# Query panels of the first block as three products, and the order of the loads around them, in a hybrid attention and expert kernel

## What is computed

```python
h = rms_norm(x, g_mix)
proj = h @ w_in
u_ssm, q, k, v, qi, ki, wi, qm, gates = jnp.split(proj, offs, axis=-1)
...
km, vm = jnp.split(rms_norm(mem, g_mem) @ w_mem_kv, 2, axis=-1)
...
merged = g_s * (y_ssm @ w_up_ssm) + g_d * (y_dsa @ w_up_dsa) + g_m * (y_mem @ w_up_mem)
x = x + merged @ w_out
...
```

## Time and profile before

| | us |
|---|---|
| median of 3 runs | 1965.04 |
| lowest, highest | 1964.48, 1965.8 |
| the profiled execution | 1964.33 |
| its span, first to last instruction | 1962.5 |

### The profile page before, as it was taken

How to read it: one execution, slowest core, us unless ns; L and a number is a source line. 1 busy time by engine, 2 the same in 40 slices (tenths; PEclk the granted TensorE clock), 3 DMA queues, 4 the chain that set the end, 5 groups by cost and what they waited for, 6 DMA issues and landing times.

```text
span 1962.5 us, 30069 instructions
## 1 busy us (share of the span) xinstructions
PE 1849.4 (94%) x12400; PEld 1424.3 (73%) x12400; DVE 1157.0 (59%) x1494; ACT 840.2 (43%) x1029; POOL 79.8 (4%) x72
## 2 busy tenths in 40 slices
PE   8998999877787779999999999999999999999998
PEld 5467886444454445888888788888888888788887
DVE  7997577433333335555687476555554688386454
ACT  5346632222121225343556645344443558555331
POOL 2642000000000000000000000000000000000000
PEclk9999999998898989999999999999999999999999
DMA  9479679999999997564454355464555445264552
GB/s 340 124 165 256 202 284 379 420 420 420 421 420 421 420 419 285 192 214 150 157 189 172 108 192 197 167 204 153 202 182 192 162 152 193 89 218 168 192 175 104
DMA packets 166921, 467.05 MB, mean 238 GB/s; under 512 B 9808, under 2 KB 21328, under 8 KB 142080
## 3 DMA queue, kind: packets, MB, share of 16 engines
q1 hardware_dynamic: 152144, 435.07, 59.8%
q0 software_dynamic: 13024, 26.81, 6.2%
q10 hardware_dynamic: 1616, 3.24, 0.5%
HBM read 557.36 MB, written 1.05 MB: 285 GB/s over the span
## 4 chain that ended last, share of the span: by engine, by line
PE 76%; DMA 19%; ACT 3%; DVE 1%; issue 1%; SPq 0%; DVEq 0%; ACTq 0%
PE ps L1042 25%; PE ps L1052 19%; PE ps L1051 19%; DMA ring<-in_w_down 12%; DMA ring<-in_w_up 5%; PE ps L1212 3%; PE ps L1557 2%; PE ps L1576 2%; PE ps L1180 1%; PE ps L1181 1%; DMA raw<-in_w_in 1%; PE ps L1281 1%; DMA raw_r<-in_w_in 1%; PE ps L1526 1%; PE ps L1337 1%
## 5 line engine op out<-in xcount | busy, mean ns | idle before, releaser
L2442 DVE TENSOR_TENSOR w_lo<-raw,w_hi 128x2048 fp32r<-128x2048 f32 x152 | 333.8, 2208 | 126.7 <-ACT w_hi L1879 118.9
L1879 ACT ACTIVATE w_hi<-raw 128x2048 fp32r<-128x2048 f32 x152 | 279.7, 1849 | 227.4 <-PE ps L1042 193.0
L1052 PE MATMUL ps<-w_hi,a_lo 128*128 128x512 f32 (+1 forms) x992 | 374.7, 378 | 0.0
L1042 PE MATMUL ps<-w_hi,a_hi 128*128 128x512 f32 (+1 forms) x960 | 367.1, 382 | 0.2 <-DVEq L2482 0.2
L1051 PE MATMUL ps<-w_lo,a_hi 128*128 128x512 f32 (+1 forms) x920 | 346.4, 377 | 0.0
L1557 PE MATMUL ps<-ring,W 128*32 128x256 f32 x3008 | 192.0, 404 | 55.9 <-DMA ring<-in_w_up 54.7
L1052 PEld LDWEIGHTS ps<-w_hi,a_lo 128*128 128x128 f32 x992 | 186.6, 188 | 34.9
L1042 PEld LDWEIGHTS ps<-w_hi,a_hi 128*128 128x128 f32 x960 | 180.7, 188 | 34.6 <-issue 2.7
L1557 PEld LDWEIGHTS ps<-ring,W 128*32 128x32 f32 x3008 | 95.5, 115 | 138.4 <-DMA ring<-in_w_up 64.7
L1051 PEld LDWEIGHTS ps<-w_lo,a_hi 128*128 128x128 f32 x920 | 173.3, 188 | 30.7 <-issue 0.2
L2442 DVE TENSOR_TENSOR y_lo<-raw,y_hi 128x2048 fp32r<-128x2048 f32 x50 | 114.6, 2292 | 48.3 <-ACT y_hi L1879 45.7
(11 more groups left out here) (479 smaller groups left out, 2858.2 us busy)
## 6 DMA issues: line engine op xcount, KB each, us to landing
ring<-in_w_gate SPq DMA_DIRECT2D x94, 1024.0 KB, 22.5
ring<-in_w_up SPq DMA_DIRECT2D x94, 1024.0 KB, 26.1
ring<-in_w_down SPq DMA_DIRECT2D x94, 1024.0 KB, 22.1
raw<-in_w_in SPq DMA_DIRECT2D x50, 1024.0 KB, 5.1
raw<-in_ffn_w_up SPq DMA_DIRECT2D x44, 1024.0 KB, 5.2
raw<-in_ffn_w_gate SPq DMA_DIRECT2D x42, 1024.0 KB, 5.1
raw<-in_ffn_w_down SPq DMA_DIRECT2D x40, 1024.0 KB, 6.0
raw<-in_w_out SPq DMA_DIRECT2D x10, 1024.0 KB, 5.0
```

Of the source, the lines that this page charges most:

```text
L1042: return released(pe.matmul(dst, a, b, skip_group_check=True, **kw))
L1052: return pe.matmul(dst, a_l, b_h, start=False, stop=final, skip_group_check=True)
L1879: act.activation(E.hi_view(name, ahead), E.raw_view(name, ahead), ACT.Copy).then_inc(hi_split, 1)
L2442: tt(E.lo_view(name, ahead), E.raw_view(name, ahead), E.hi_view(name, ahead).bitcast(F32), ALU.subtract)\
```

## The change

The q and qm units join `CAST_UNITS` ahead of the gates: `scan_piece` multiplies them by `split_products` and waits for the split rows of x (`gate_rows_rest`) and for the unit's accumulating load; SP no longer loads them. The slots of the cast loads are now a table, `CAST_SLOT`, and a load into a slot waits for the unit that last had it. The negations of ACT and the transfers of POOL are placed anew: POOL has one accumulating load ahead of each of tiles 5, 8, 9, 10, 14 and 15 and a cast load ahead of each of tiles 11, 12 and 14. The small loads except the constants and the scan parameters go from ACT's queue to SP's, behind u and km. Late in ACT's order the copies of the turned probabilities come ahead of the copies of gate 3.

```diff
@@ -59,8 +59,9 @@
 PRE_SPLIT = [("up", br, c) for br in ("ssm", "dsa", "mem") for c in range(2)] + [(("wo", c), kh) for c in range(2) for kh in range(2)]
-CAST_UNITS = [(("gate", c), kh) for c in range(6) for kh in range(2)]
+CAST_UNITS = ([(n, kh) for n in ("q", "qm") for kh in range(2)] + [(("gate", c), kh) for c in range(6) for kh in range(2)])
 CAST_SLOTS = 5
+CAST_SLOT = [0, 1, 2, 3, 4, 0, 1, 2, 3, 4, 0, 1, 2, 3, 0, 1]
 IN2 = dict(qa=(0, 512), kva=(512, 256), qb=(768, 512), kb=(1280, 512), vb=(1792, 1024),
@@ -122,6 +123,11 @@
         self.n = start + per * trips
+
+
+def cast_before(j):
+    same = [i for i in range(j) if CAST_SLOT[i] == CAST_SLOT[j]]
+    return len(same), same[-1] if same else None

@@ -819,7 +825,7 @@

-                slot = CAST_UNITS.index(name) % CAST_SLOTS
+                slot = CAST_SLOT[CAST_UNITS.index(name)]
                 hi = [*(w_hi[:, i] for i in range(RAW)), w_lo[:, RAW - 1], a_hi[:, :, :].rearrange("p k s -> p (k s)")][slot]
@@ -957,9 +963,23 @@

+            def small_loads(name):
+
+                if name == ("u", 0):
+                    sp.dma_start(head_rows, A["head_rows"].partition_broadcast(P)).then_inc(rows_loaded, 16)
+                if name == ("u", 1):
+                    sp.dma_start(cc.rearrange("p a t c -> p (a t c)"), A["ssm_c"]).then_inc(c_loaded, 16)
+                    sp.dma_start(bn.rearrange("p a t c -> p (a t c)"), A["ssm_b"]).then_inc(b_loaded, 16)
+                    sp.dma_start(xn[:, :, :], A["mem"].rearrange("a (t p) d -> p (a t) d", p=P)).then_inc(mem_loaded, 16)
+                if name == ("km", 0):
+                    with nc.allow_non_contiguous_dma(reason="positions as a column"):
+                        sp.dma_start(posi[:, :], A["positions"].rearrange("a (t p) -> p (a t)", p=P)).then_inc(pos_loaded, 16)
+                    sp.dma_start(pos_row_i, A["positions"][0].partition_broadcast(P)).then_inc(pos_loaded, 16)
+
             for name in stretch1:
...
                     pre_load(name)
+                small_loads(name)
                 if units.at[name][0] + 1 == gates_used + PRE_RAW:
@@ -1131,9 +1151,22 @@
                     bank((n, t))
+                w, b, dst = unit_shape[name][1], E.pre_view(name), ps[:, bank_of[(n, t)], :]
+                if name in CAST_UNITS:
+                    if t == 0:
+                        pe.wait_ge(gate_rows_rest, 16)
+                        pe.wait_ge(rest_loaded[E.pre_slot(name)], E.pre_loads(name))
+                    hi_, lo_ = E.cast_halves(name)
+                    for k in range(4):
+                        at = (slice(None), 4 * kh + k, slice(t * P, t * P + P))
+                        m = split_products(dst[:, 0:w], g_hi[at], g_lo[at], hi_[:, k, :], lo_[:, k, :], kh == k == 0, kh == 1 and k == 3)
+                    if t == 1:
+                        unit_done()
+                    if kh == 1:
+                        fill(m, (n, t))
+                    return
                 if t == 0:
                     raw_unit(name)
-                w, b, dst = unit_shape[name][1], E.pre_view(name), ps[:, bank_of[(n, t)], :]
                 if n == "km":
@@ -1861,13 +1894,6 @@
             act.dma_start(par[:, 0:3], A["ssm_params"].rearrange("p (a t) -> p a t", a=3)).then_inc(par_loaded, 16)
-            act.dma_start(head_rows, A["head_rows"].partition_broadcast(P)).then_inc(rows_loaded, 16)
-            with nc.allow_non_contiguous_dma(reason="positions as a column"):
-                act.dma_start(posi[:, :], A["positions"].rearrange("a (t p) -> p (a t)", p=P)).then_inc(pos_loaded, 16)
-            act.dma_start(pos_row_i, A["positions"][0].partition_broadcast(P)).then_inc(pos_loaded, 16)
-            act.dma_start(bn.rearrange("p a t c -> p (a t c)"), A["ssm_b"]).then_inc(b_loaded, 16)
-            act.dma_start(xn[:, :, :], A["mem"].rearrange("a (t p) d -> p (a t) d", p=P)).then_inc(mem_loaded, 16)
-            act.dma_start(cc.rearrange("p a t c -> p (a t c)"), A["ssm_c"]).then_inc(c_loaded, 16)

@@ -1881,7 +1907,7 @@
                 n0 = PRE_SPLIT.index(name)
-                earlier = PRE_SPLIT[n0 - RAW] if n0 >= RAW else CAST_UNITS[(7, 10, 11)[n0]]
+                earlier = PRE_SPLIT[n0 - RAW] if n0 >= RAW else CAST_UNITS[(12, 14, 15)[n0]]
                 act.wait_ge(unit_used, E.unit_value(earlier) + 1)
@@ -1891,7 +1917,7 @@
                 j = CAST_UNITS.index(name)
-                act.wait_ge(cast_loaded[j % CAST_SLOTS], j // CAST_SLOTS * 16 + 16)
+                act.wait_ge(cast_loaded[CAST_SLOT[j]], cast_before(j)[0] * 16 + 16)
                 act.wait_ge(unit_used, n0 + 1 - PRE_RAW)
@@ -1988,6 +2014,8 @@
                              scale=r_of["mem" if n in ("km", "vm") else "x"][:, t:t + 1])
+                if i == 0:
+                    minus(("q", 0))
                 if i in (1, 2):
@@ -1996,10 +2024,13 @@
                     act.activation(g_lo[:, :, :], g_hi.bitcast(F32), ACT.Copy, scale=-1.0).then_inc(gate_rows_negated, 1)
+                    minus(("q", 1))
+                    minus(("qm", 0))
                 if i == 2:
+                    minus(("qm", 1))
                     minus((("gate", 0), 0))
+                if i == 3:
                     minus((("gate", 0), 1))
-                if i == 3:
                     minus((("gate", 1), 0))
@@ -2081,8 +2112,8 @@
             minus((("gate", 5), 0))
+            probs_out("dsa", 0, 4, probsT)
             gate(3)
-            probs_out("dsa", 0, 4, probsT)
             minus((("gate", 5), 1))
@@ -3623,9 +3654,9 @@

-                name, slot = CAST_UNITS[j], j % CAST_SLOTS
-                if j >= CAST_SLOTS:
-                    pool.wait_ge(unit_used, units.at[CAST_UNITS[j - CAST_SLOTS]][0] + 1)
+                name, slot = CAST_UNITS[j], CAST_SLOT[j]
+                if cast_before(j)[0]:
+                    pool.wait_ge(unit_used, units.at[CAST_UNITS[cast_before(j)[1]]][0] + 1)
                 pool.dma_start(E.cast_halves(name)[0], unit_source(name, {})).then_inc(cast_loaded[slot], 16)
@@ -3643,8 +3674,25 @@
                         .then_inc(gate_rows_rest, 16)
-                if T in (9, 11, 13):
-                    add_raw((T - 9) // 2)
+                if T == 5:
+                    add_raw(0)
+                if T == 8:
+                    add_raw(1)
+                if T == 9:
+                    add_raw(2)
+                if T == 10:
+                    add_raw(3)
+                if T == 11:
+                    pool.wait_ge(gate_rows_rest, 16)
+                    pool.wait_ge(unit_used, E.unit_value(("kvi", 1)) + 1)
+                    cast_load(4)
+                if T == 12:
+                    cast_load(5)
+                if T == 14:
+                    add_raw(4)
+                    cast_load(6)
+                if T == 15:
+                    add_raw(5)
                 pool.wait_ge(done["scanned"], nth("scanned", T))
@@ -3655,15 +3703,13 @@

-            pool.wait_ge(gate_rows_rest, 16)
-            pool.wait_ge(unit_used, E.unit_value(("qm", 1)) + 1)
-            cast_load(CAST_SLOTS - 1)
-            add_raw(3)
-            cast_load(CAST_SLOTS)
-            for j in range(4, len(CAST_UNITS)):
+            add_raw(6)
+            cast_load(7)
+            cast_load(8)
+            for j in range(7, len(CAST_UNITS)):
+                add_raw(j)
                 if j + 2 < len(CAST_UNITS):
                     cast_load(j + 2)
-                add_raw(j)

```

## The result

The changed kernel takes 1991.84 us at the median (1989.18 to 1992.35), the kernel before 1965.42 us (1964.48 to 1966.51), four runs of each on the same chip: a ratio of 1.0135, 95% interval 1.0123 to 1.0147. The change costs 26.4 us, where the prediction said 17; the time lies 0.8 us above its range. Direction and mechanism held, the size did not. The lowest of the four runs, 1989.18, is inside the range: that the median is just outside may be chance, that it is 10 us above the forecast is not. The profiled execution's span is 1990.5 us, 28.0 longer than before.

What follows compares the result with a forecast made beforehand. TensorE and VectorE were taken as full before 120 us, with TensorE's shift carried to the end. Waits, with savings inside, made 15.7 us, clock 1.7: 17.4 later, forecast 1982 us; term bounds 1974 to 1991, stated range 1968 to 1991.

Steps and rivals of the forecast that it cites:

- What bounds it: Before 120 us TensorE and VectorE are full; a TensorE shift before 300 us reaches the end neither grown nor shrunk.
- Start: At u's product: fewer loads share the DMA, so u's second half starts sooner; gain 1.5 us (0.5 to 1.85).
- The products: At q and qm: a unit takes 5.67 us instead of 7.1; four units save 5.6 us of TensorE.
- Wait 1: Before q, at about 80 us: TensorE waits 3.5 us (2 to 5) for the split rows' transfer.
- Waits 2 and 3: Late casts delay negations ahead of q's and qm's copies: TensorE waits 7.8 us before qm; VectorE's head work starts 15.8 late.
- The clock: In the first stretch: one loss at reduced clock after the new waits, 1.7 us (0 to 5).
- Gate 0 during wait 3: While VectorE waits for qm's copy, TensorE runs gate 0 to about 142 us, then waits for the head rows.
- Behind that: After the head rows: gate 5's negation ahead of the probabilities' copies makes second scores 16.7 us late, then 15.7 late.
- (1): Faster: casts are down before ScalarE needs them, as the scan does not hold POOL; 1958 to 1961 us, chance 0.06.
- (2): No change: wait before qm halved, next small, gate 0's accumulating loads offset the saving; 1961 to 1969 us, chance 0.06.
- (3): Smaller loss: cast 6 lands before qm is full; gate 0's accumulating loads still hold TensorE; 1969 to 1974 us, chance 0.09.
- (4): Larger loss: POOL's queue after the scan sets each later gate, negations hold ScalarE; above 1991 us, chance 0.06.

Runs made afterwards that it cites:

- e12: Changed kernel with only q as products, qm raw, copies before negations, rows' transfer at tile 5, q's first accumulating load at tile 3, late orders restored: 1961.26 us.
- e4: Changed kernel with gate 0's sums in banks 2 and 3 instead of 4 and 5, the banks qm fills: 1990.65 us.
- e5_rows_early: Changed kernel with the transfer of the split rows issued at scan tile 5 instead of 7: 1987.18 us.
- e2_loads_only: Kernel before with only the small loads moved from ACT's queue to SP's: 1965.24 us.
- e1_copies_first: Changed kernel with ScalarE's copies of q ahead of gate 0's negations and copies of qm ahead of gate 1 half 0's negation: 1980.87 us.
- e6_warm: Changed kernel with 44 unused products of the identity into a free bank where TensorE waits for the copy of qm: 1990.49 us.
- e3: Changed kernel with the negation of gate 5 half 0 moved behind the copies of the turned probabilities: 1987.06 us.
- e10: Kernel before with the probabilities' copies ahead of gate 3's copies and, after the scan, each POOL accumulating load ahead of the next cast: 1968.90 us.
- e7: Changed kernel with copies ahead of gate 0 and 1 negations, rows' transfer at tile 5, gate 5 half 0's negation behind the probabilities' copies: 1975.05 us.
- e8: e7 with POOL's cast and accumulating loads also issued earlier, such as cast 4 a tile sooner: 1969.93 us.
- e9_swap_only: Kernel before with only the copies of the turned probabilities moved ahead of the copies of gate 3: 1965.20 us.

## Why the prediction was wrong

Landmarks, in us of the profiled execution:

| | forecast | after |
|---|---|---|
| start gained | 1.5 | 0.36 |
| first q product | 84.0 | 85.22 |
| cast 4 issued, landed | 99.9, 106.6 | 103.38, 110.34 |
| first qm product | 109.2 | 112.91 |
| cast 6 issued, landed | 121.3, 131.3 | 127.19, 137.62 |
| head work begins | 134.6 | 141.09 |
| head rows turned | 147.1 | 156.53 |
| second scores | 202.9 | 213.18 |
| later at the end | 17.4 | 28.0 |

**What bounds it; the shift carried to the end.** Right. TensorE's first product with the ring is at 309.25 us before and 337.01 in after, 27.8 later, and the span is 28.0 longer; e12's is at 306.14, 3.1 sooner, its span 3.0 shorter. It holds within about 1 us: in e4 that product is 0.7 sooner than in after and the span 0.6 longer.

**Start, 1.5 forecast, 0.36 measured.** The first km product starts at 29.30 where it was 29.66. The term was sized by how much sooner u's second half could begin, at the rate of DMA. x landed no sooner (TensorE starts on it at 7.23 us and not 7.29). u did begin sooner (10.67 us, not 11.33) and its second weights landed well ahead, but its 15.05 us in one piece ended only 0.4 sooner. This term lay outside its own bounds by 0.1 us. What lacks is in the pace of u's first products; why it differs is not shown. The same start in the profile of e5_rows_early:

```profile
10.73 13.98 PE L1062 MATMUL ps<-a_full,raw 128*128 128x256 f32 x64
```

From 11 to 13 us after's stage table has 4 records of TensorE in each us, e5's 6, though both have 1.00 as the clock there. In e5 the first km product starts at 28.29 us, 1.4 sooner than before: nearly the forecast. In the profiles of the eleven kernels with this start it starts at 28.29 to 29.72, 0.75 sooner in the mean than the 29.7 of the three with the old one. So the term was not far off on what the loads allow, and what is seen of it varies from execution to execution; the median of e2_loads_only shows none of it.

**The products.** Right: 96.67 to 102.34 is 5.67 us a unit at full clock, as forecast.

**Wait 1.** Right: 3.53 us where 3.5 was forecast.

**Waits 2 and 3.** The mechanism was right in each link, and so was the price of each link: from the first q product to cast 4's issue 15.9 us forecast, 18.2 measured, a difference that the slow q unit (2.9, below) more than covers; issue to landing 6.7 and 7.0 for cast 4, 10.0 and 10.4 for cast 6; waits 7.8 and 7.6 us. e1_copies_first shows the cause by undoing it. The estimate of 4.4 us for 1 MB from the Trainium skill, DMA: Bandwidth & Descriptors, section "Anatomy of one DMA", is not borne out by these traces: the quickest cast took 6.2 us, and this one 6.96.

**The clock, the step that failed.** One loss of 1.7 us was put into the sum, for one of the four waits, though the text named new waits of 3.5 to 8 us in plural. There were four: the q unit at 85.22 took 8.5 us in place of 5.7 (2.9), the qm unit 8.4 (112.91 to 121.27; 2.7), gate 0's first 7.9 (2.2), and the second scores with the first three products behind them 4.8 in place of 2.7 (2.1): 9.9 us where 1.7 were put in. The first two are in the ring and also made the casts later; e5_rows_early shows this for the first, the second is read from the rows alone. The third was worth 1.7 in the profile of e6_warm. It should have been one loss for each new wait, with the measured stretch behind each: even the bound of 5 was for one. How long the stretch is, is in part luck: behind the same wait of 3.5 or 3.6 us before q it lasts 6.8 us in after, e3 and e4 and 3.4 us in e1 and e6, where the q unit loses 1.6 us and not 2.9.

**Gate 0 during wait 3, a step that was wrong.** TensorE did not run gate 0 while VectorE was held, because gate 0's banks are those of qm. Gate 0 began with the copy, at 141.19, and reached the head rows at 156.53; at full clock (2.2 us less) it would have been 154.3, still 1.6 us behind the head rows at 152.7. In e4_gate0_banks the head rows hold TensorE instead, and no gain can be told.

**Behind that.** 2.5 us were put in for the negation ahead of the copies, less the waits that go, so that the shift grew by 1.5 from the head rows on. It grew by 4.4 (23.6 to 28.0): the wait before the scores was 6.85 us, where before has 1.97, and the clock loss behind it is 2.1 of it. The mechanism is shown by e3 and, in the kernel before, by e10.

**The sum.** The landmarks say where the 10.6 us that were missing came in: 1.2 up to the first q product (the start); 2.3 up to cast 4's issue and 2.2 from the first qm product to cast 6's issue, where the two units at half clock are 2.9 and 2.7 and the other prices were 0.6 and 0.5 too high; 0.8 in landings and copies; 2.9 up to the head rows, which TensorE reached 3.8 us after VectorE had them (gate 0's slow unit 2.2, its bank 1.6), while VectorE's work was 0.9 shorter than forecast; 0.8 up to the second scores; 0.3 behind them, over the 1.7 that the forecast had there for the clock. That adds up to 10.6 but for rounding. Of it, the clock term is 6.0 without the third stretch and 8.2 with it.

**Rivals.** (1) and (2) fell: ScalarE copied q at 112.18 us, and VectorE began at 141.09. (3) came true in part, and only in e1 and e7, where gate 0 waits 4.2 us for its accumulating load, but with other waits behind it that (3) did not have. (4) has the time, above 1991, but only a part of its mechanism: behind the head rows a negation does hold ScalarE longer than forecast, while no gate of after waits over 0.3 us for its accumulating load. The load of POOL's queue shows where the rest is mended: in e8 8.8 us of TensorE's waits are for accumulating loads.

## What to carry to other kernels

An engine's queue is in order: before putting an operation that waits for a transfer ahead of one that frees a bank or feeds another engine, follow who starts that transfer and whether it waits, by any path, for the very work that is held back; here the two were a ring, which cost twice and drew in four engines. Count what each new wait of TensorE costs twice: its length, and a stretch at half clock behind it, which cost from 1.6 to about 3 us each time here that a wait was 2.8 us or longer. Take the half of the change that has its inputs anyway: two units instead of four, with their loads placed before anything else in the queue needs it, gained 3 us where the whole lost 26.

## What the runs showed of the hardware

The half clock followed every idle time of TensorE of 2.8 to 10.5 us in the first 300 us. (Behind the 7.2 us ahead of its first product the stage table has the full clock, though u's first products were slow, as said of the start.) Behind those of 1.6 to 2.4 us it came in some executions and not in others: the 2.37 and 1.97 us of before have full clock behind them, while 2.15 us at the same place in e9_swap_only, 2.25 in e2_loads_only, 2.38 in e12_q_placed and 1.75 in e5_rows_early were followed by half clock. It came while TensorE was still idle or up to 1.1 us after it had resumed, and lasted for 3.4, 6.8 or 10.2 us. In six of the other kernels a stretch of 3.4 us also begins between 295 and 322 us, with no idle time of TensorE over 0.3 us in it or just before; why is not shown. Products that compute nothing, put in the gap, kept the clock at full (e6).

Two transfers of POOL's queue issued close together take longer: a casting or accumulating MB alone takes 6.2 to 8.6 us, the cast issued 0.8 us behind an accumulating load 10.4, and the accumulating load issued 0.6 us behind the rows' transfer 14.7. What they share is not shown. An accumulating load holds POOL for less time than its record has: in after its tile 10 starts 0.8 us behind the start of such a load (98.79 to 99.61), whose record lasts 1.30 us; the prediction took 1.3.
